# Both steps of the gated delta rule inverted level by level together, four groups at once, and the convolution's taps spread over twice as many turns

## The chip, the cores and the metric

One core of a Trainium2 chip runs the kernel. The metric is the device time of one execution in microseconds (us). Engines are named as in the profile: PE (TensorE, matmuls and transposes), DVE (VectorE), ACT (ScalarE), POOL (GpSimd), and SP, which only issues DMAs. Each engine works through its own list of instructions strictly in order; they meet at semaphores.

## What is computed

Two transformer blocks on 256 tokens of width 1024. The first has two layers (`DEPTH` = 2) with a hybrid mixer each; the change is in that mixer:

```
def hybrid_mixer(x, ...):
    proj = x @ w_in
    p_conv, p_q, p_k, p_v, p_dn, p_z, p_b, p_a = split_projection(proj)
    c = c_lin * jax.nn.sigmoid(c_gate)
    c = depthwise_conv(c, conv_dw) + conv_dw_b            # 31 taps, 256 channels
    y_conv = jax.nn.silu(layer_norm(c, ...)) @ conv_pw
    y_diff = differential_attention(q, k, v, lam, ...)    # 4 heads
    y_dn = gated_deltanet_bidir(p_dn, p_z, p_b, p_a, ...) # 4 heads, forward and backward
    return jnp.concatenate([y_conv, y_diff, y_dn], axis=-1) @ w_o
```

The delta rule is solved in blocks ("steps") of 128 tokens. For each step, direction and head a triangular 128x128 matrix has to be inverted. The inverse X is built up in seven levels (`LEVELS` = 7): level k takes the part LM of the matrix L that a constant mask of level k selects, and computes P = LM·X, then X − X·P, then the transpose of the new X. Layer 1 is followed by a feed-forward net, layer 2 by eight experts; a second block follows.

## The kernel before

**Groups.** The four heads of one step and one direction are a group, held in one PSUM bank as 4 x 128 columns. There are four groups in a layer: i = 2·step + dr. Before the change two `Group` objects (one for each direction) serve both steps, so step 1 can begin only when step 0's buffers are free.

**Threads and turns.** Each engine's list for the mixer is written by `weave`, which takes one piece in turn from each of three generators: `mixer_attention`, `mixer_delta`, `mixer_conv`. A `yield` ends a piece. I call one round of `weave` a turn and count turns from 0; turn n of one engine belongs to turn n of the others. Nothing else decides the order: inside a turn attention comes first, then delta, then conv.

**Delta on PE** (`invert`): k = 0 transposes LM (L809). Each level k from 1 takes three turns, each for both directions: P = LM·X (8 matmuls, L759), then X·P (L759), then the transposes of X (L838). ACT copies P and the transpose out of PSUM (L2141), DVE subtracts X·P from X (L1314), and POOL makes the next level's LM with `mask` (L2622). Before the first level POOL also makes `XT` = 1 − LM and the first mask, four operations for each pair of groups. The delta thread takes 50 turns: begin 2, products 2, scaled 2, invert 18, solved 1, begin 2, then products and invert of step 1 (20 turns, with state(0) and scaled(1) beside them), solved 1, state(1) 2.

**Attention**: turns 0 to 3 project the keys (L567, w_in slice at ring use `MIX[l]`+4), turns 4 to 7 the values and the rotated heads' transposes (L574). From turn 8 each of the eight head-and-tile pieces i has its turn of `scores(i)` (L676; turn 8 + 3i), and in the turn after it `turn_mix(i-1)` (L574, which needs DVE's mixing of i-1), and in the third turn `out` (L567). On DVE, in the turn of scores(i): the maxima of scores(i) (L1517), then the mixing of i-1 (L1524, L1317, L1314, L1320). From turn 41 PE does pieces of the output projection (L720).

**Convolution** on DVE: 30 taps for two halves, 60 operations (L1320 on b_cols), four a turn, so 15 turns. They are followed on PE by two sums (L567 with b_cst 128x256) and by the pointwise matmuls (L567 with b_pw), with DVE, POOL and ACT in between.

**Weights** come through four ring slots (`ring`), in the order of `uses`; SP waits for the readers of what lay in the slot, in that order. The slot of use `MIX[l]`+4 (the keys' weights) is next filled with the first weights of the feed-forward net or of the experts.

```
def weave(*threads):
    live = list(threads)
    while live:
        for g in list(live):
            try:
                next(g)
            except StopIteration:
                live.remove(g)
```

Of the kernel before, what the change touches and what calls it, by code (L numbers as in the profile page):

```python
# [238 lines left out]
class Views:  # L239


    def __init__(self, arena):
        self.arena, self.at = arena, 0

    def __call__(self, *shape):
        n = int(np.prod(shape))
        ap = self.arena[:, self.at:self.at + n]
        self.at += n
        assert self.at <= 23168, self.at
        return view(ap, *shape)  # L250


class Group:


    def __init__(self, A, XTf, n):
        self.LT, self.LM, self.P, self.X, self.XT = (A(4, 128) for _ in range(5))
        self.QT = [A(4, 128), view(XTf[:, 512 * n:512 * n + 512], 4, 128)]
        self.Rv, self.Rk, self.kd, self.U = (A(4, 64) for _ in range(4))
        self.wT, self.st, self.g4 = A(2, 128), A(2, 128), [A(16), A(16)]  # L260


def two_blocks(nc, a):
    ctx = ExitStack()
    with ctx:
# [24 lines left out]
        with nc.sbuf_tensor("b_arena", [128, 23168], F32) as arena:  # L290
            pass
# [51 lines left out]
        groups = [Group(A, XTf, n) for n in range(2)]  # L343
        q2 = view(flat(groups[0].P), 2, 256)
        r8 = groups[0].g4[0][:, 0:8]
# [74 lines left out]
        r_one, r_out = sig("r_one", 4), sig("r_out", 4)  # L420
# [62 lines left out]
        def mixer_uses(l):  # L483
# [5 lines left out]
            use(rows8(w, 1024, 512), k_rows(l, 1))  # L489
# [72 lines left out]
        def pe(e):  # L562
# [161 lines left out]
            def mixer_conv(l):  # L724
                for _ in range(15):
# [15 lines left out]
            def mixer_delta(l, done):  # L741
# [20 lines left out]
                def begin(step):  # L762
                    for dr in range(2):
                        i, t = 2 * step + dr, step if dr == 0 else 1 - step
                        G, tri, g4 = groups[dr], C(f"tri{dr}"), gz[:, t, 4 * dr:4 * dr + 4]
# [10 lines left out]
                def products(step):  # L776
                    for dr in range(2):
                        i, t = 2 * step + dr, step if dr == 0 else 1 - step
                        G = groups[dr]
# [16 lines left out]
                def scaled():  # L796
                    for dr in range(2):
                        yield

                def invert(step):  # L800
                    for k in range(LEVELS):
                        last = k == LEVELS - 1
                        for dr in range(2):
                            G, i = groups[dr], 2 * step + dr
                            b = B.take()
                            e.wait_ge(*masked(l, 14 * step + 2 * k + dr))
                            if k == 0:
                                for h in range(4):
                                    ins = e.transpose(heads(b)[:, h, :], G.LM[:, h, :], ident)  # L809
                                ins.then_inc(lm_turn.sem)  # L810
                                B.until(b, inv_X0(l, i))
                            else:
# [2112 lines left out]
```

## Time and profile before

| | |
|---|---|
| median of 3 runs | 2388.54 us (2385.37 to 2389.2) |
| profiled execution, its own time | 2390.41 us |
| its span | 2388.3 us |
| mean granted TensorE clock | 0.954 of full |
| PE, DVE, ACT, POOL busy | 91%, 59%, 48%, 54% of the span |

The two mixers' woven parts run from 76 to about 277 us and from 565 to about 768 us. The rest of the span is the feed-forward net, the experts and the second block, which are not touched. PE's busy time counts the modelled ends of matmuls, so what matters in the mixer is the gaps in it and what ended them.

### The profile page before, as it was taken

The numbers are of one execution on the slowest core, as the hardware profiler recorded it, in microseconds if no ns is written. First come the engines' busy times: TensorE is split into PE (matmuls) and PEld (weight loads), VectorE is DVE, ScalarE is ACT, GpSimd is POOL, SyncE is SP. The second block draws the span as 40 slices with busy tenths as digits, with TensorE's granted clock in tenths as the row PEclk, the third lists the DMA queues.
The fourth block names the chain that finished last, engine by engine and source line by source line (L and its number), as shares of the span: only waits on it lengthen the run. The fifth ranks groups of instructions, "written<-read, shape, count | busy, mean of one in ns | idle before, by whom it ended". The sixth has DMA issues, their size and how long they took to land.

```text
span 2388.3 us, 26921 instructions
## 1 busy us (share of the span) xinstructions
PE 2175.7 (91%) x10612; PEld 1742.4 (73%) x10612; DVE 1408.6 (59%) x1743; ACT 1144.9 (48%) x1164; POOL 1296.4 (54%) x555
## 2 busy tenths in 40 slices
PE   8988699989788599999999999999899996887997
PEld 7467488875675577787777777888778774647997
DVE  1774534345844477777777776433477775545665
ACT  1143244321431376767767675433376672534554
POOL 0333145502430398989989896455399891204453
PEclk9999899999989699999999999999999997978999
DMA  8210075433100499998989897445489893204550
GB/s 295 106 36 1 1 263 191 159 121 134 36 1 1 156 354 334 349 358 322 358 315 361 317 361 270 176 177 204 149 318 356 322 358 132 99 26 159 212 199 32
DMA packets 208097, 484.97 MB, mean 203 GB/s; under 512 B 9168, under 2 KB 13008, under 8 KB 206928
## 3 DMA queue, kind: packets, MB, share of 16 engines
q1 hardware_dynamic: 207952, 483.02, 55.9%
q8 instruction: 92, 1.51, 0.3%
q14 instruction: 53, 0.43, 0.1%
HBM read 481.96 MB, written 1.05 MB: 202 GB/s over the span
## 4 chain that ended last, share of the span: by engine, by line
PE 82%; DVE 11%; ACT 2%; issue 2%; SPq 1%; POOL 1%; DMA 1%; DVEq 0%; ACTq 0%
PE bank L938 20%; PE bank L940 20%; PE bank L939 20%; PE bank L567 10%; PE bank L759 4%; DVE b_arena L1320 3%; PE bank L574 3%; DVE b_arena L1314 2%; PE bank L720 1%; DVE b_X L1314 1%; ACT e_hi L2141 1%; PE bank L1207 1%; POOL e_lo L2762 1%; DMA b_ba<-in_w_in 1%; DVE b_arena L1317 1%
## 5 line engine op out<-in xcount | busy, mean ns | idle before, releaser
L2762 POOL TENSOR_TENSOR e_lo<-b_ring,e_hi 128x512 fp32r<-128x512 f32 (+2 forms) x407 | 1146.0, 2837 | 569.8 <-ACT e_hi L2141 569.8
L1772 DVE TENSOR_TENSOR e_lo<-b_ring,e_hi 128x1536 fp32r<-128x1536 f32 (+1 forms) x403 | 773.6, 1920 | 471.0 <-ACT e_hi L2141 467.7
L2141 ACT ACTIVATE e_hi<-b_ring 128x2048 fp32r<-128x2048 f32 (+1 forms) x407 | 776.4, 1911 | 367.5 <-PE bank L940 334.7
L938 PE MATMUL bank<-e_hi,e_xh 128*128 128x512 f32 (+1 forms) x1200 | 476.2, 397 | 30.8 <-issue 13.0
L940 PE MATMUL bank<-e_hi,e_xl 128*128 128x512 f32 (+1 forms) x1200 | 467.4, 390 | 0.0
L939 PE MATMUL bank<-e_lo,e_xh 128*128 128x512 f32 (+1 forms) x1200 | 466.7, 389 | 0.0
L938 PEld LDWEIGHTS bank<-e_hi,e_xh 128*128 128x128 f32 x1200 | 226.8, 189 | 97.5 <-issue 50.3
L938 PE MATMUL bank<-e_hi,e_th 128*128 128x512 f32 x688 | 272.2, 396 | 0.7
L940 PE MATMUL bank<-e_hi,e_tl 128*128 128x512 f32 x688 | 268.6, 390 | 0.0
L939 PE MATMUL bank<-e_lo,e_th 128*128 128x512 f32 x688 | 268.3, 390 | 0.0
L940 PEld LDWEIGHTS bank<-e_hi,e_xl 128*128 128x128 f32 x1200 | 226.9, 189 | 48.1
L939 PEld LDWEIGHTS bank<-e_lo,e_xh 128*128 128x128 f32 x1200 | 227.1, 189 | 42.2
L2622 POOL TENSOR_TENSOR b_arena<-b_arena,b_cst 128x512 f32<-128x512 f32 (+1 forms) x72 | 90.9, 1280 | 218.9 <-DVE b_arena L1314 121.0
L2141 ACT ACTIVATE b_arena<-bank 128x512 f32<-128x512 f32 (+2 forms) x164 | 87.1, 547 | 212.8 <-PE bank L574 80.0
L938 PEld LDWEIGHTS bank<-e_hi,e_th 128*128 128x128 f32 x688 | 129.1, 188 | 39.0 <-issue 11.2
L940 PEld LDWEIGHTS bank<-e_hi,e_tl 128*128 128x128 f32 x688 | 129.1, 188 | 27.9
L939 PEld LDWEIGHTS bank<-e_lo,e_th 128*128 128x128 f32 x688 | 129.3, 188 | 23.7
L759 PEld LDWEIGHTS bank<-b_arena 128*128 128x128 f32 (+1 forms) x928 | 120.5, 205 | 21.1 <-issue 15.6
L759 PE MATMUL bank<-b_arena 128*128 128x128 f32 (+1 forms) x928 | 132.3, 294 | 3.6 <-issue 1.6
L567 PE MATMUL bank<-b_ring,b_XT 128*128 128x512 f32 (+1 forms) x320 | 121.6, 532 | 2.4 <-issue 2.4
L2622 POOL TENSOR_TENSOR b_arena<-b_arena 128x256 f32<-128x256 f32 (+1 forms) x46 | 36.7, 821 | 157.6 <-ACT b_arena L2141 136.8
L938 PE MATMUL bank<-e_xh,e_hi 128*128 128x256 f32 x384 | 110.1, 287 | 1.4 <-DVE e_xl L1776 1.4
(214 smaller groups left out, 2426.4 us busy)
## 6 DMA issues: line engine op xcount, KB each, us to landing
b_ring<-in_moe_w SPq DMA_DIRECT2D x168, 2048.0 KB, 8.1
b_ring<-in_w_in SPq DMA_DIRECT2D x15, 2048.0 KB, 8.1
b_ring<-in_ffn_w SPq DMA_DIRECT2D x15, 2048.0 KB, 7.9
b_ring<-in_w_up SPq DMA_DIRECT2D x12, 2048.0 KB, 8.0
b_ring<-in_w_down SPq DMA_DIRECT2D x6, 2048.0 KB, 8.5
b_ring<-in_w_o SPq DMA_DIRECT2D x4, 2048.0 KB, 7.8
b_gain<-in_gains SPq DMA_DIRECT2D x7, 1024.0 KB, 4.9
b_ring<-in_w_out SPq DMA_DIRECT2D x2, 2048.0 KB, 8.3
```

The lines of the kernel that those rows point to most:

```text
L567: ins = e.matmul(out, x, y, start=start and i == 0, stop=stop and i == len(pairs) - 1)
L574: last = e.transpose(out[:, tok(j)], x, ident)
L759: last = e.matmul(heads(b)[:, h, :], *f(h), start=True, stop=True)
L938: e.matmul(out, ah, bh, start=first, stop=False)
L939: e.matmul(out, ah, bl, start=False, stop=False)
L940: return e.matmul(out, al, bh, start=False, stop=last)
L1314: return e.tensor_tensor(out, x, y, op)
L1320: return e.scalar_tensor_tensor(out=out, in0=x, scalar=s, in1=y, op0=o1, op1=o2)
L1772: e.tensor_tensor(lo[:, 0:at], raw[:, 0:at], r32(hi[:, 0:at]), ALU.subtract).then_inc(lo_dve.sem)
L2141: return e.activation(out, x, ACT.Copy)
L2622: return e.tensor_tensor(out, x, y, op)
L2762: e.tensor_tensor(lo[:, at:], raw[:, at:], r32(hi[:, at:]), ALU.subtract).then_inc(lo_pool.sem)
```

## The change

The `Group` objects become four for each layer: two in the arena, and two whose four large tiles lie in the ring slot of the keys' weights and whose XT lies in the first half of `b_XT`. Both steps' `begin` and `products` come first (turns 0 to 7), then one `invert` for all four groups: each level has two turns of P (step 0's pair, then step 1's), two of X·P, two of transposes. `solved`, `state(0)` and `state(1)` follow. That makes 49 turns. On POOL `scaled` is dealt out into the X·P turns. The taps come two a turn, in 30 turns, and what follows them is 15 turns later. The ring slot is now filled again only after the last X·P (`inv_XP(l)`).

```diff
@@ second groups, in the ring slot and in XT
+        first = [Group([A(4, 128) for _ in range(4)], A(4, 128), A) for _ in range(2)]
+        def second(l):
+            r = ring[(MIX[l] + 4) % NR]
+            return [Group([view(r[:, 2048 * n + 512 * i:2048 * n + 512 * i + 512], 4, 128) for i in range(4)],
+                          view(XTf[:, 512 * n:512 * n + 512], 4, 128), B, first[n]) for n in range(2)]
@@ mixer_uses
-            use(rows8(w, 1024, 512), k_rows(l, 1))
+            use(rows8(w, 1024, 512), inv_XP(l))
@@ pe, mixer_conv
-                for _ in range(15):
+                for _ in range(30):
@@ pe, mixer_delta (DVE, ACT and POOL alike)
-                def invert(step):
+                def invert():
                     for k in range(LEVELS):
                         last = k == LEVELS - 1
-                        for dr in range(2):
...
-                        yield
+                        for step in range(2):
+                            for dr in range(2):
+                                i = 2 * step + dr
+                                G, n = groups[l][i], 4 * (k - 1) + i
+                                b = B.take()
+                                e.wait_ge(*masked(l, 4 * k + i))
...
+                            yield
@@
-                yield from begin(0)
-                yield from products(0)
-                yield from scaled()
-                yield from invert(0)
-                yield from solved(0)
-                yield from begin(1)
-                yield from turns(middle(), tail())
-                yield from solved(1)
+                for step in range(2):
+                    yield from begin(step)
+                    yield from products(step)
+                yield from invert()
+                yield from solved()
+                yield from state(0)
                 yield from state(1)
@@ dve, mixer_conv
-                    if i % 2:
-                        yield
+                    yield
@@ pool, mixer_delta
                         if step:
-                            e.wait_ge(*X_out(l, 10 + dr))
+                            e.wait_ge(*k_rows(l))
...
+                    rest = scaled()
...
+                                if k == 0:
+                                    G = groups[l][i]
+                                    if step:
+                                        e.wait_ge(*v_rows(l))
+                                    e.wait_ge(*masked(l, i))
+                                    tt(G.XT, id4, G.LM, ALU.subtract).then_inc(inv_XT0.sem)
+                                    e.wait_ge(*lm_turn(l, i))
+                                    e.wait_ge(*inv_XT0(l, i))
+                                    mask(i, 1)
+                                elif not last:
+                                    e.wait_ge(*inv_P(l, 4 * (k - 1) + i))
+                                    mask(i, k + 1)
+                            yield
...
+                        for step in range(2):
+                            next(rest, None)
+                            yield
```

How PE's list reads in layer 1, within level k = 2. Before, from the two products P over the turn of scores to `turn_mix` (L759 is a product, L676 the scores, L574 `turn_mix`; both directions come in each place):

```order
L759 MATMUL bank<-b_arena 128x128 [waits s_X_out,s_masked]
L759 MATMUL bank<-b_arena 128x128 x3
L759 MATMUL bank<-b_arena 128x128 [waits s_X_out,s_masked]
L759 MATMUL bank<-b_arena 128x128 x3
L676 MATMUL bank<-b_arena 128x256 [waits s_s_exp]
L676 MATMUL bank<-b_arena 128x256 [waits s_score]
L759 MATMUL bank<-b_arena 128x128 [waits s_XT_out,s_P_out]
L759 MATMUL bank<-b_arena 128x128 x3
L759 MATMUL bank<-b_arena 128x128 [waits s_XT_out,s_P_out]
L759 MATMUL bank<-b_arena 128x128 x3
L574 MATMUL bank<-b_cst,b_arena 128x128 [waits s_s_mix,s_s_exp]
L574 MATMUL bank<-b_cst,b_arena 128x128
```

After, one turn of scores among the transposes (L690 is the scores, L852 the transposes, L588 `turn_mix`):

```order
L690 MATMUL bank<-b_arena 128x256 [waits s_s_exp]
L690 MATMUL bank<-b_arena 128x256 [waits s_score]
L852 MATMUL bank<-b_cst,b_arena 128x128 [waits s_X_out]
L852 MATMUL bank<-b_cst,b_arena 128x128 x3
L852 MATMUL bank<-b_cst,b_arena 128x128 [waits s_X_out]
L852 MATMUL bank<-b_cst,b_arena 128x128 x3
L588 MATMUL bank<-b_cst,b_arena 128x128 [waits s_s_mix,s_s_exp]
L588 MATMUL bank<-b_cst,b_arena 128x128
```

Between scores and `turn_mix` there stood always the two X·P products; now there stand in turn the two P products of step 1's pair and, as here, the two short transposes.

On POOL, from the first masks to the first level, before (each operation on 128x512 takes the same form; L2622 is every tensor operation of POOL):

```order
L2622 TENSOR_TENSOR b_arena<-b_cst,b_arena 128x512 [waits s_masked]
L2622 TENSOR_TENSOR b_arena<-b_arena,b_cst 128x512 [waits s_inv_XT0,s_lm_turn]
L2622 TENSOR_TENSOR b_arena<-b_cst,b_arena 128x512 [waits s_masked]
L2622 TENSOR_TENSOR b_arena<-b_arena,b_cst 128x512 [waits s_inv_XT0,s_lm_turn]
L2622 TENSOR_TENSOR b_arena<-b_arena,b_cst 128x512 [waits s_inv_P] x8
```

and after:

```order
L2610 TENSOR_TENSOR b_ring0<-b_ring0,b_cst 128x512 [waits s_L_out] x2
L2610 TENSOR_TENSOR b_arena<-b_cst,b_arena 128x512 [waits s_masked]
L2610 TENSOR_TENSOR b_arena<-b_arena,b_cst 128x512 [waits s_inv_XT0,s_lm_turn]
L2610 TENSOR_TENSOR b_arena<-b_cst,b_arena 128x512 [waits s_masked]
L2610 TENSOR_TENSOR b_arena<-b_arena,b_cst 128x512 [waits s_inv_XT0,s_lm_turn]
L2610 TENSOR_TENSOR b_XT<-b_cst,b_ring0 128x512 [waits s_masked,s_v_rows]
L2610 TENSOR_TENSOR b_ring0<-b_ring0,b_cst 128x512 [waits s_inv_XT0,s_lm_turn]
L2610 TENSOR_TENSOR b_XT<-b_cst,b_ring0 128x512 [waits s_masked,s_v_rows]
L2610 TENSOR_TENSOR b_ring0<-b_ring0,b_cst 128x512 [waits s_inv_XT0,s_lm_turn]
```

Eight such operations now stand in one row behind the last mask of `products`, where four stood in each of two places.

On DVE, between two turns of scores, before (L1517 the maxima, L1320 on b_cols the taps):

```order
L1320 SCALAR_TENSOR_TENSOR b_arena<-b_arena,b_cols 128x251 [waits s_dve_order] x2
L1320 SCALAR_TENSOR_TENSOR b_arena<-b_arena,b_cols 128x250 [waits s_dve_order] x2
L1320 SCALAR_TENSOR_TENSOR b_arena<-b_arena,b_cols 128x249 [waits s_dve_order] x2
L1517 TENSOR_REDUCE b_arena<-bank 128x2 [waits s_score]
L1317 TENSOR_SCALAR b_arena<-b_arena 128x2 [waits s_dve_order]
L1524 RECIPROCAL b_arena<-b_arena 128x2 [waits s_s_exp]
```

and after:

```order
L1326 SCALAR_TENSOR_TENSOR b_arena<-b_arena,b_cols 128x255 [waits s_dve_order] x4
L1541 COPY b_arena<-bank 128x128 [waits s_att_sq]
L1326 SCALAR_TENSOR_TENSOR b_arena<-b_arena,b_cols 128x254 [waits s_dve_order] x2
L1523 TENSOR_REDUCE b_arena<-bank 128x2 [waits s_score]
L1323 TENSOR_SCALAR b_arena<-b_arena 128x2 [waits s_dve_order]
L1530 RECIPROCAL b_arena<-b_arena 128x2 [waits s_s_exp]
```

There are six taps between two scores instead of twelve.

## Rows read from the trace of the kernel before

**Rows 1.** First line of the profile's page
```profile
span 2388.3 us, 26921 instructions
```

**Rows 2.** Busy time in stretches, both mixers; start:end, length, each engine
```profile
core 0: us, PE busy (x) PEld busy (x) DVE busy (x) ACT busy (x) POOL busy (x), PEclk, DMA share, GB/s
...
76.00:277.00 201.00, 175.79 (x975) 128.74 (x976) 116.69 (x255) 59.10 (x139) 61.97 (x58) 0.96 0.09 32
565.00:768.00 203.00, 178.04 (x980) 129.65 (x980) 116.65 (x258) 59.08 (x139) 63.30 (x58) 0.96 0.09 32
```

**Rows 3.** PE's waits in the first mixer (75 to 277 us): total, times, longest
```profile
PE bank L574 <- DVE b_arena L1320: 8.5, 5, 2.8
PE bank L574 <- DVE b_arena L1314: 4.6, 2, 3.4
PE bank L574 <- ACT b_arena L2240: 2.7, 1, 2.7
```

**Rows 4.** Timeline of PE, turns 5 and 6: start, length, idle before
```profile
111.19 1.97 PE L574 MATMUL bank<-b_cst,b_arena 128*128 128x128 f32 x8 [3.35 <-DVE b_arena L1314]
...
118.28 1.10 PE L574 MATMUL bank<-b_cst,b_arena 128*128 128x128 f32 x8 [1.23 <-DVE b_arena L1314]
```

**Rows 5.** Timeline of PE, level 2 of step 0
```profile
130.01 1.23 PE L838 MATMUL bank<-b_cst,b_arena 128*128 128x128 f32 x8 [1.18 <-DVE b_arena L1314]
131.07 1.95 PE L759 MATMUL bank<-b_arena 128*128 128x128 f32 x16
132.95 1.45 PE L676 MATMUL bank<-b_arena 64*128 64x256 f32 x4
134.33 2.05 PE L759 MATMUL bank<-b_arena 128*128 128x128 f32 x16
...
139.18 0.41 PE L574 MATMUL bank<-b_cst,b_arena 128*128 128x128 f32 x2 [2.79 <-DVE b_arena L1320]
```

**Rows 6.** Timeline of DVE: taps, then a mixing's last operation
```profile
82.86 1.61 DVE L1320 SCALAR_TENSOR_TENSOR b_arena<-b_arena,b_cols 128x241 f32<-128x241 f32 x4
...
121.06 7.41 DVE L1320 SCALAR_TENSOR_TENSOR b_arena<-b_arena,b_cols 128x253 f32<-128x253 f32 x8
...
130.38 6.80 DVE L1320 SCALAR_TENSOR_TENSOR b_arena<-b_arena,b_cols 128x254 f32<-128x254 f32 x12
...
138.54 0.48 DVE L1320 SCALAR_TENSOR_TENSOR b_arena<-b_arena 128x256 f32<-128x256 f32 x1
```

**Rows 7.** Timeline of POOL: before the first level, then two masks
```profile
118.66 1.27 POOL L2622 TENSOR_TENSOR b_arena<-b_cst,b_arena 128x512 f32<-128x512 f32 x1
...
122.92 1.27 POOL L2622 TENSOR_TENSOR b_arena<-b_arena,b_cst 128x512 f32<-128x512 f32 x1
124.66 2.74 POOL L2622 TENSOR_TENSOR b_arena<-b_arena,b_cst 128x512 f32<-128x512 f32 x2 [0.47 <-PE bank L759]
```

**Rows 8.** Timeline of PE: scores and `turn_mix` with no taps on DVE
```profile
181.44 1.45 PE L676 MATMUL bank<-b_arena 64*128 64x256 f32 x4
...
185.00 0.41 PE L574 MATMUL bank<-b_cst,b_arena 128*128 128x128 f32 x2 [0.59 <-DVE b_arena L1320]
```

**Rows 9.** Timeline of DVE, a mixing while POOL works (197 to 201 us)
```profile
197.37 0.69 DVE L1517 TENSOR_REDUCE b_arena<-bank 128x2 f32<-128x512 f32 x1
...
198.46 0.59 DVE L1317 TENSOR_SCALAR b_arena<-b_arena 128x256 f32<-128x256 f32 x1
198.98 0.56 DVE L1314 TENSOR_TENSOR b_arena<-b_arena,b_sc 128x1 f32<-128x1 f32 x1
199.57 1.45 DVE L1320 SCALAR_TENSOR_TENSOR b_arena<-b_arena 128x256 f32<-128x256 f32 x1
```

**Rows 10.** Timeline of PE: the `turn_mix` behind that mixing
```profile
201.17 0.41 PE L574 MATMUL bank<-b_cst,b_arena 128*128 128x128 f32 x2 [2.82 <-DVE b_arena L1320]
```

**Rows 11.** Timeline of PE: the convolution's second sum, and its pointwise product
```profile
159.70 1.03 PE L567 MATMUL bank<-b_arena,b_cst 128*128 128x256 f32 x4
...
168.35 1.97 PE L567 MATMUL bank<-b_arena,b_pw 128*128 128x256 f32 x8 [0.55 <-ACT b_arena L2144]
```

**Rows 12.** Timeline of SP's queue: the first feed-forward weights
```profile
96.90 27.18 SPq L2809 DMA_DIRECT2D b_ring<-in_ffn_w  x2
```

**Rows 13.** Timeline of PE: the mixer's last product, and what follows
```profile
272.42 7.13 PE L567 MATMUL bank<-b_ring,b_arena 128*128 128x512 f32 x16 [0.47 <-ACT b_arena L2141]
```

**Rows 14.** The page's DMA issues: KB of one, us to landing
```profile
b_ring<-in_ffn_w SPq DMA_DIRECT2D x15, 2048.0 KB, 7.9
```

More of the change, by code:

```diff
@@ L841, in invert @@
-                        yield
+                        for step in range(2):
+                            for dr in range(2):
+                                G, n = groups[l][2 * step + dr], 4 * (k - 1) + 2 * step + dr
+                                b = B.take()
+                                e.wait_ge(*X_out(l, n))
+                                for h in range(4):
+                                    ins = e.transpose(heads(b)[:, h, :], G.X[:, h, :], ident)
+                                ins.then_inc(inv_turn.sem)
+                                B.until(b, XT_out(l, n))
+                            yield
@@ L2340, in invert, with solved @@
-                        yield
-                def solved(step):
-                    for dr in range(2):
+                        for step in range(2):
+                            for dr in range(2):
+                                b = B.take()
+                                e.wait_ge(*inv_turn(l, 4 * (k - 1) + 2 * step + dr))
+                                copy(groups[l][2 * step + dr].XT, heads(b)).then_inc(XT_out.sem)
+                            yield
+                def solved():
+                    for i in range(4):
@@ L2359, in state @@
                     yield
-                def tail():
-                    yield from state(0)
-                    yield from scaled()
-                def middle():
-                    yield from products(1)
-                    yield from invert(1)
-                yield from begin(0)
-                yield from products(0)
-                yield from scaled()
-                yield from invert(0)
-                yield from solved(0)
-                yield from begin(1)
-                yield from turns(middle(), tail())
-                yield from solved(1)
+                for step in range(2):
+                    yield from begin(step)
+                    yield from products()
+                yield from invert()
+                yield from solved()
+                yield from state(0)
                 yield from state(1)
@@ L2724, in invert @@
                         yield
[L2726 to L2746 removed]
+                        yield
+                for step in range(2):
+                    yield from begin(step)
+                    yield from products(step)
+                yield from invert()
             def mixer(l):
```

341 lines of the change are left out of this document (149 added, 192 removed).

## The prediction, made before the changed kernel had run

> **What bounds the kernel now.** The page's first line gives the span, 2388.3 us [rows 1]; the execution's own time was 2390.41 us, 1.9 us above the median of the runs (2388.54). Next I read busy time by stretches, to see which engine leaves how much open in the part that the change touches. In the first mixer PE is busy 175.8 of 201 us and in the second 178.0 of 203 [rows 2], no other engine above 117. So PE has some 25 us of gaps in each mixer. The products that it does are the same ones after the change, and the number of turns goes only from 50 to 49. The whole effect is therefore what becomes of about 25 us of gaps in each of two layers (and of the clock within them): even with all of it gone the kernel would be 50 us faster, and a part of it (the start, the tail) is not touched.
>
> The third view is who ended PE's waits. The largest entries of the first mixer are waits for DVE, and they stand in front of L574 [rows 3]: the attention's `turn_mix` and the rotated heads, not the inversion. In front of the inversion's own products stand few. In other words, the dependency chain of the inversion (PE, ACT, PE, DVE, PE) is already covered, by the two directions and the attention piece of each turn. What is not covered is the attention's own chain: scores on PE, maxima and mixing on DVE, `turn_mix` on PE in the next turn.
>
> The timeline shows how. In a level with taps, scores run from 132.95, the two X·P products to 136.4, and then PE is idle for 2.79 us, until DVE has mixed [rows 5]; in that time DVE was still in twelve taps, 6.80 us from 130.38 on [rows 6]. Where DVE has no taps in front, `turn_mix` starts 2.1 us after the end of scores (182.89 to 185.00) [rows 8]. That 2.1 us is the bare chain. X·P for two directions lasts 2.05 us [rows 5], so before the change it covers the bare chain almost exactly, and only taps make a gap of it.
>
> **The change, term by term**, for one mixer, in us of PE idle time. I replay PE's list turn by turn with the durations of the rows.
>
> *Front, turns 0 to 7.* Before: gaps of 0.84 at the start, 3.35 and 1.23 [rows 4], 5.4 in all. After, the rotated heads still wait for DVE in turn 5 (same chain, 3.4). Behind them comes `begin(1)`, whose wide copy on POOL now stands behind POOL's two rotary operations; these start when PE's wait ends and take 2.8, the copy 0.6, while PE has 2.3 of work: a gap of 1.1. In turn 6 the second rotary wait has `begin(1)`'s four DVE operations in front of it: 1.6 in place of 1.23. Sum 7.0, so +1.6. Bounds: 0 (POOL and DVE quick enough) and +3.
>
> *Start of the levels.* POOL needs four operations for each pair of groups (XT and mask), 5.5 us from 118.66 to 124.19 [rows 7]. Now eight stand in a row behind the last mask of `products`, which can start only about when turn 7 ends: 1 + 11.1 us. PE's work from there to the end of the fourth P is 1.45 (scores), 2.1 (transposes), 1.95, 1.45, 1.95 = 8.9 [rows 5]; its last product waits for POOL's last mask. Gap 4.2. Before, step 0's wait was covered by the values' projection, and step 1's was mostly paid by a `turn_mix` wait of 2.8 [rows 10] and 1.7 behind it. Bounds: 2.5 and 6.
>
> *Scores among P.* Four turns of scores (i = 1, 3, 5, 7) now have the two P products behind them, 1.95 us, nearly the bare chain: 0.4 would be left. But at that time POOL is making masks: each P product that ends starts one, 2.74 for two [rows 7]. The trace shows what DVE's mixing costs beside POOL: the three operations from 198.46 on take 0.59, 0.56 and 1.45 [rows 9], where the last alone takes 0.48 [rows 6], and PE's gap behind it was 2.82 with 1.1 us of cover [rows 10]. That is 1.6 us more than the bare chain. Taps show the same: 1.61 for four with POOL idle, 7.41 for eight with POOL at work [rows 6]. Before, masks were over when the mixing began, since they belong to the turn ahead. I take 2.0 for each, 8.0 in all; bounds 0.4 each (no meeting with POOL) and 2.4.
> The Trainium skill bears on this (SBUF — State Buffer, section "Who interferes with whom"): a DVE instruction with two SBUF inputs and a GpSimd instruction that reads SBUF exclude each other for a whole instruction. By that rule the mixing's two operations of this kind could each wait for a whole mask and these four gaps be near 3 us each, 4 us more in a mixer than I take; the rows, which show 1.6 us, decide here.
>
> *Scores among transposes.* The other turns (i = 2, 4, 6) have the two transposes as their only cover, 1.04 to 1.23 us [rows 5] where X·P stood: 1.1 of the bare chain is left open, and DVE comes 0.25 late from the subtraction of the last X·P and two taps. I take 1.35, the first 0.5 more: 4.5. Bounds 3 and 8.
>
> *What the taps gave.* With six taps and not twelve between two scores, DVE is no longer behind in the levels: the waits of 2.79 and 2.7 and smaller ones go. Before, all gaps between turn 8 and the tail sum to 16.6 (24.5, the sum of the wait list, less 5.4 at the front and 2.5 in the tail). All of these are taken away and replaced by the terms here.
>
> *Behind the taps.* The pointwise product waits for a chain from the second sum's end (160.6 to 168.35, 7.8 us) [rows 11], in which ACT loads two tables. PE had 7.3 of work in that time and a gap of 0.55; after, the turns are two single-pair P, one transposition and no scores, 5.8: gap 2.0 (bounds 0.5 and 2.5). The norm of the attention rows stays as it is, at 2.2.
>
> *Tail.* `state(0)` moves from the middle to the end: PE's work is only moved, one wait of 0.4 is added; 2.9 in place of 2.5.
>
> *The ring slot.* The first weights of the next stage were issued at 96.9 [rows 12] and will be issued after the last X·P, near 255. Two loads, which share this queue and its order, need 2 x 7.9 us to land [rows 14], so about 271; the mixer's last product ends at 279.6 [rows 13] and only then does ACT begin to split them. Zero; if that cover were gone it would be up to 16 us once in each layer.
>
> Sum after: 7.0 + 4.2 + 8.0 + 4.5 + 2.0 + 2.2 + 2.9 = 30.8, against 24.5: **+6.3 a mixer, +12.6 in all.** Against its own time 2390.4 + 12.6 = 2403.0, and 1.9 below that for the median: **2401 us**. The bounds of all terms at once give 18 to 40, that is -13 to +31 in all, but they do not fall together.
>
> The clock: the granted clock is 0.96 over each mixer [rows 2]. At two levels, 1.2 and 2.4 GHz, that is 8% of 201 us, 16 us, at the lower one, which lost 8 us. They lie behind the gaps of 2.7 us and more (the first L574 of rows 4 took 1.97, the second, of the same form, 1.10). After, single gaps are smaller but more of them; I take the same loss.
>
> **Rivals.**
> 1. *Faster.* The gaps among P come out at 0.4 since the mixing slips between two masks (-13 for both layers: no change), and in addition the clock stays high, since only two gaps above 2.7 are left in a mixer (up to -8 in each). Time 2378. For it: gaps of 2.8 disappear and PE is evenly loaded at 80%. Against it: the rows of POOL and DVE at 198 us, and the long gap at the start of the levels. Chance 0.22.
> 2. *No change.* Half of this: gaps of 1.2 among P, or a third of the clock's loss back. 2389. Chance 0.18.
> 3. *Much slower.* DVE falls behind in the turns after the start, where POOL works without a break for 11 us and slows the taps to 0.9 each; each later turn_mix starts late, and gaps of 3 bring the clock down in the levels: 8 us more in each mixer. 2418. For it: eight taps took 7.41. Against it: DVE has half the taps. Chance 0.08.
> 4. *The weights come late.* SP's queue holds the second load behind the first, and both now wait for the inversion. It decides once they land after 279.6, that is with 8 us more than I count: 2410 to 2430. Chance 0.02.
> My forecast (slower by 0.25 to 0.9%) has 0.50.
>
> **From these to the numbers.** The likeliest case's own range is 2394 to 2410. To leave out no more than 2 in 10 it has to take in the second case and most of the first: 2378 to 2413. A measurement of this kernel can tell about 0.2%, 4.8 us, from no change. Faster 0.22, within it 0.18, slower 0.60.
>
> **What the changed profile would show.** Woven parts of some 207 us and 209 us with PE busy as before and about 31 of gaps. PE's waits still led by L588 (`turn_mix`) for DVE, with more and smaller entries: seven in each mixer of 1.2 to 2.4. On POOL eight operations in a row, and behind them two PE waits at the first P products. DVE's stretches of 6.8 us of taps gone. In the mixing among P, a last operation of 1.2 to 1.45; if it is 0.48 there, rival 1 gains. Granted clock about 0.96 in the mixers; at 0.99 the forecast is wrong by 8 to 12 us. The ffn weights issued near 255 us and no new wait of ACT behind the mixer.

## The result, and the profile after

The changed kernel takes 2399.53 us (median of 5 runs, 2398.31 to 2404.46) against 2388.54 (2385.37 to 2389.76, 5 runs): 11 us slower. The ratio estimated from all the runs is 1.0052, 95% interval 1.0038 to 1.0067. The forecast was slower, 2401 us. The profiled execution took 2398.31 us of its own.

The page's first line, and busy time over the woven parts; each stretch runs from the mixer's first product behind the 0.84 us wait to the start of its last (L581 here, L567 in [rows 13]). Columns as in [rows 2]:

```profile
span 2396.2 us, 26907 instructions
...
76.12:279.38 203.26, 170.58 (x964) 127.60 (x965) 123.88 (x253) 55.43 (x137) 57.87 (x51) 0.94 0.09 32
572.09:773.39 201.30, 169.19 (x964) 126.37 (x964) 123.82 (x253) 55.22 (x137) 57.90 (x51) 0.95 0.09 32
```

Cut the same way, the parts of before are 196.3 and 194.9 us, with PE busy 171.2 and 170.9. PE's work has not grown; the gaps in it have. The sum of the gaps that the timeline marks is 31.6 and 31.1 us now and was 23.8 and 22.7. PE's waits in the first mixer, 75 to 285 us, which answer to [rows 3]:

```profile
PE bank L588 <- DVE b_arena L1326: 17.3, 8, 5.8
PE bank L581 <- ACT b_arena L2140: 3.6, 1, 3.6
PE bank L588 <- DVE b_arena L1320: 3.2, 1, 3.2
PE bank L773 <- DVE b_arena L1320: 2.6, 1, 2.6
PE bank L773 <- POOL b_ring L2656: 2.0, 2, 1.7
```

`turn_mix` (L588) waiting for DVE's mixing (L1326) leads, with twice what the same wait had before. Where each gap stands, in PE's timeline:

```profile
112.70 1.09 PE L588 MATMUL bank<-b_cst,b_arena 128*128 128x128 f32 x8 [3.18 <-DVE b_arena L1320]
116.02 2.05 PE L773 MATMUL bank<-b_cst,b_ring 128*128 128x128 f32 x8 [1.73 <-POOL b_ring L2656]
...
140.62 3.27 PE L773 MATMUL bank<-b_arena 128*128 128x128 f32 x16 [2.64 <-DVE b_arena L1320]
...
153.76 0.66 PE L588 MATMUL bank<-b_cst,b_arena 128*128 128x128 f32 x2 [5.81 <-DVE b_arena L1326]
...
163.37 0.41 PE L588 MATMUL bank<-b_cst,b_arena 128*128 128x128 f32 x2 [1.10 <-ACT b_arena L2236]
...
172.42 0.41 PE L588 MATMUL bank<-b_cst,b_arena 128*128 128x128 f32 x2 [2.17 <-DVE b_arena L1326]
...
222.49 3.19 PE L581 MATMUL bank<-b_arena,b_pw 128*128 128x256 f32 x8 [3.58 <-ACT b_arena L2140]
...
233.56 1.08 PE L588 MATMUL bank<-b_cst,b_arena 128*128 128x128 f32 x4 [2.54 <-DVE b_arena L1326]
```

From 163 us on the gaps alternate, 1.10 among the transposes and 2.17 or 2.18 among the products P, three of each. The second mixer has the same list to within 0.2 us, except that the 1.73 is 0.74 there. What is new in the size is the 5.81. DVE's timeline in front of it, then a mixing among P (168 to 172 us):

```profile
142.88 1.27 DVE L1320 TENSOR_TENSOR b_ring<-b_cst,bank 128x512 f32<-128x512 f32 x2
144.08 5.73 DVE L1326 SCALAR_TENSOR_TENSOR b_arena<-b_arena,b_cols 128x250 f32<-128x250 f32 x4
149.73 0.68 DVE L1523 TENSOR_REDUCE b_arena<-bank 128x2 f32<-128x512 f32 x1
...
169.56 1.22 DVE L1320 TENSOR_TENSOR b_arena<-b_arena,b_sc 128x1 f32<-128x1 f32 x1
170.82 1.45 DVE L1326 SCALAR_TENSOR_TENSOR b_arena<-b_arena 128x256 f32<-128x256 f32 x1
```

and POOL's timeline over the same times:

```profile
144.06 1.26 POOL L2610 TENSOR_TENSOR b_XT<-b_cst,b_ring 128x512 f32<-128x512 f32 x1
145.46 1.26 POOL L2610 TENSOR_TENSOR b_ring<-b_ring,b_cst 128x512 f32<-128x512 f32 x1
146.69 2.85 POOL L2610 TENSOR_TENSOR b_arena<-b_arena,b_cst 128x512 f32<-128x512 f32 x2
149.50 2.65 POOL L2610 TENSOR_TENSOR b_ring<-b_ring,b_cst 128x512 f32<-128x512 f32 x2
...
169.44 2.55 POOL L2610 TENSOR_TENSOR b_ring<-b_ring,b_cst 128x512 f32<-128x512 f32 x2 [0.47 <-PE bank L773]
```

A tap takes 0.40 us with POOL idle (1.61 for four, [rows 6]) and 1.43 here, where POOL runs without a pause: one DVE operation for each of POOL's. An operation on one element a row (128x1), 0.15 us elsewhere, takes 1.22 at 169.56 and ends as POOL's first mask of that pair does; the next ends 0.3 us after the second mask. DVE's subtractions that read PSUM (x2 in 1.27) are not slower.

### The profile page after: what moved, and what is told of

Its sections match the earlier page's. It is cut to its first block, busy times and chain, and to the rows that moved or that the text cites. A ratio compares the mean times of both kernels' runs of the same rounds, so it can differ in the third digit from the quotient of the medians.

```text
span 2396.2 us, 26907 instructions
## 1 busy us (share of the span) xinstructions
PE 2166.2 (90%) x10612; PEld 1736.7 (72%) x10612; DVE 1426.3 (60%) x1743; ACT 1138.0 (47%) x1162; POOL 1287.1 (54%) x543
## 4 chain that ended last, share of the span: by engine, by line
PE 81%; DVE 11%; issue 2%; POOL 2%; ACT 2%; SPq 1%; DMA 1%; DVEq 0%; ACTq 0%; POOLq 0%
PE bank L944 20%; PE bank L946 19%; PE bank L945 19%; PE bank L581 11%; PE bank L773 3%; PE bank L588 3%; DVE b_arena L1326 2%; DVE b_arena L1320 2%; POOL b_arena L2610 1%; PE bank L734 1%; ACT e_hi L2137 1%; DVE b_X L1320 1%; POOL e_lo L2742 1%; PE bank L1213 1%; DVE b_arena L1323 1%
## 5 line engine op out<-in xcount | busy, mean ns | idle before, releaser
L2610 POOL TENSOR_TENSOR b_arena<-b_arena,b_cst 128x512 f32<-128x512 f32 (+1 forms) x44 | 55.5, 1282 | 167.1 <-DVE b_arena L1320 99.1
L2137 ACT ACTIVATE b_arena<-bank 128x512 f32<-128x512 f32 (+2 forms) x120 | 60.3, 529 | 166.9 <-PE bank L588 61.2
L581 PE MATMUL bank<-b_ring,b_XT 128*128 128x512 f32 (+1 forms) x320 | 125.8, 545 | 2.4 <-issue 2.4
L2610 POOL TENSOR_TENSOR b_arena<-b_arena 128x256 f32<-128x256 f32 (+1 forms) x34 | 26.3, 786 | 166.0 <-ACT b_arena L2137 136.8
L946 PE MATMUL bank<-e_xh,e_lo 128*128 128x256 f32 x384 | 108.7, 283 | 0.0
L945 PE MATMUL bank<-e_xl,e_hi 128*128 128x256 f32 x384 | 108.7, 283 | 0.0
```

The costliest lines, as they stand in the source:

```text
L581: ins = e.matmul(out, x, y, start=start and i == 0, stop=stop and i == len(pairs) - 1)
L945: e.matmul(out, ah, bl, start=False, stop=False)
L946: return e.matmul(out, al, bh, start=False, stop=last)
L2137: return e.activation(out, x, ACT.Copy)
L2610: return e.tensor_tensor(out, x, y, op)
```

## The experiments

All times are medians beside the kernel before on the same chip (its medians there were 2388.1 to 2390.0); the ratio is estimated from the runs of both and is not exactly that of the medians. The woven parts, their gaps, PE's busy time and its granted clock in them are from the profiled execution of each, first and second mixer. The last column is the rest of that execution's span, where no edit changes what the engines do.

| | us | ratio to before (95%) | woven parts | gaps | PE busy | clock | rest |
|---|---|---|---|---|---|---|---|
| before | 2388.54 | | 196.3, 194.9 | 23.8, 22.7 | 171.2, 170.9 | 0.96, 0.96 | 1997.1 |
| changed | 2399.53 | 1.0052 (1.0038 to 1.0067) | 203.3, 201.3 | 31.6, 31.1 | 170.6, 169.2 | 0.94, 0.95 | 1991.6 |
| e1 | 2385.63 | 0.9992 (0.9980 to 1.0004) | 197.2, 199.0 | 17.9, 19.6 | 177.5, 177.6 | 0.91, 0.91 | 1995.1 |
| e2 | 2411.5 | 1.0093 (1.0076 to 1.0109) | 206.6, 208.6 | 33.3, 31.0 | 172.4, 176.7 | 0.93, 0.91 | 1993.8 |
| e3 | 2382.89 | 0.9966 (0.9954 to 0.9979) | 192.7, 192.3 | 21.0, 20.5 | 170.2, 170.5 | 0.95, 0.95 | 1999.2 |
| e4 | 2392.95 | 1.0017 (1.0006 to 1.0028) | 196.0, 197.5 | 24.8, 25.6 | 170.1, 170.9 | 0.95, 0.95 | 1996.2 |
| e5 | 2403.82 | 1.0053 (1.0037 to 1.0069) | 199.8, 200.2 | 30.1, 30.1 | 168.7, 169.1 | 0.95, 0.94 | 2005.2 |
| e6 | 2388.86 | 0.9990 (0.9978 to 1.0001) | 191.7, 190.8 | 23.3, 22.9 | 167.4, 166.9 | 0.96, 0.96 | 2000.1 |
| e7 | 2373.05 | 0.9926 (0.9913 to 0.9938) | 188.4, 188.7 | 20.5, 20.7 | 167.0, 167.0 | 0.97, 0.97 | 1996.9 |
| e8 | 2382.71 | 0.9972 (0.9961 to 0.9982) | 191.1, 191.6 | 20.9, 20.7 | 169.4, 169.9 | 0.96, 0.96 | 1993.8 |
| e9 | 2373.35 | 0.9934 (0.9921 to 0.9947) | 185.8, 190.2 | 21.4, 20.9 | 163.4, 168.4 | 0.98, 0.96 | 2003.0 |
| e10 | 2385.22 | 0.9981 (0.9972 to 0.9989) | 189.8, 190.1 | 20.0, 20.2 | 168.9, 168.9 | 0.96, 0.96 | 1996.3 |
| e11 | 2372.73 | 0.9942 (0.9927 to 0.9957) | 187.6, 188.8 | 17.7, 18.9 | 169.0, 168.9 | 0.96, 0.96 | 1993.6 |
| e12 | 2372.09 | 0.9925 (0.9909 to 0.9942) | 185.2, 185.2 | 18.9, 18.6 | 165.3, 165.5 | 0.97, 0.97 | 1999.7 |

Two columns are easy to overlook. PE does the same products in all rows, yet its busy time goes from 163 to 178 us with the clock that it is granted, so a woven part can shrink or grow without its gaps. And the rest, which no edit touches, differs by up to 13.6 us between the profiled executions, more than the change costs; a difference of a few us between two medians says little of the woven parts unless the profile shows it there.

The theory was that of the prediction: the joint inversion costs by what it puts beside what. A `turn_mix` gets less cover on PE, and its mixing on DVE now meets POOL's masks. The rivals were that the dependency chain of the inversion itself or the clock sets the time.

**The change in halves.** e1 is the kernel before with the taps alone spread:

```diff
-                    if i % 2:
-                        yield
+                    yield
@@ pe, mixer_conv
-                for _ in range(15):
+                for _ in range(30):
```

> The kernel before, with the taps alone changed: two a turn in 30 turns, and what follows them 15 turns later; the two steps are still inverted one after the other. My theory: PE's gaps in the mixer are waits for the attention's mixing on DVE, and before the change the taps made those at 139 and 149 us (2.8, 2.7), with 0.8 and part of 1.2 beside them. Then this half of the change is a gain: some 4.5 us less of gaps in each mixer, 2379 to 2382 us. Rival A (the taps sat in time that DVE had to spare): 2388. Rival B (the taps only move: they now slow DVE in the start of step 1's levels, where POOL is busy, and the scores of turn 29): 2386 to 2392, with a longer wait than 2.8 at that place.

The time is unchanged, close to rival B, whose longer wait came as well. The gaps of [rows 5] and their like are gone and two new ones are there, 3.62 (a mixing beside POOL's operations at the start of step 1's levels) and 3.65 (a subtraction behind DVE's chain for the convolution's norm). The gaps are still 5.9 us less in the first mixer and 3.1 in the second, but PE's busy time rose from 171.2 to 177.5 and from 170.9 to 177.6: the granted clock ate the gain (last section).

e2 is the changed kernel with that edit undone, four taps a turn in 15 turns:

> The changed kernel with the taps alone undone: four a turn in 15 turns. My theory: the joint inversion alone is what costs, and the taps' spreading had taken part of it back, so this is slower still: DVE has four taps a turn in the start of the levels, where POOL slows each to about 1.4 us, so the gap of 5.8 us there grows by 3 to 6; later turns have no taps and gain 0.3 each. 2403 to 2410 us. Rival (taps are innocent in the changed kernel): 2398 to 2401.

12 us slower than the changed kernel, slower than the forecast of 2403 to 2410. The gaps at the start of the levels are 5.44 and 6.63 in place of 2.64 and 5.81, and the next is 2.80. The last waits behind scores are those of the changed kernel (2.19, 1.10, 2.18), but one gap among transposes and the 3.58 in front of the pointwise product, which comes earlier here, are gone. In sum the gaps are 33.3 and 31.0, only 1.7 us more in the first mixer and none in the second, while the woven parts are 3.3 and 7.3 us longer, at a clock of 0.93 and 0.91 and with PE busy 1.8 and 7.5 us more. So the joint inversion alone costs some 22 us, and the spread taps take half of that back, but less through the gaps, as my theory had it, than through the clock.

**Do the masks cause the gaps among P?** e3 is the changed kernel with the masks of levels 2 to 6 made one element wide, so that the products of those levels use what lies in LM already:

```diff
+                    if k > 1:
+                        tt(G.LM[:, 0, 0:1], G.LT[:, 0, 0:1], C(f"m{1 - i % 2}{k}")[:, 0:1], ALU.mult).then_inc(masked.sem)
+                        return
                     tt(G.LM, G.LT, M, ALU.mult).then_inc(masked.sem)
```

> The changed kernel with POOL's masks of levels 2 to 6 reduced to one element each, in place of 128x512; so it leaves out that part of the computation (the inverse is wrong), and POOL is nearly idle in the levels. It tells whether the gaps of 2.2 us behind scores among P are made by POOL's masks beside DVE's mixing. My theory: they fall to 0.4 to 0.6 (the bare chain of 2.1 less 1.95 of P products), and the gap of 5.8 by 1 to 3; those of 1.1 behind scores among transposes stay. 2384 to 2390 us. Rival (the chain itself is that long and POOL has no part): gaps stay at 2.2, 2399.

PE's gaps in it, 152 to 206 us:

```profile
152.53 0.41 PE L588 MATMUL bank<-b_cst,b_arena 128*128 128x128 f32 x2 [3.03 <-DVE b_arena L1326]
...
161.73 0.41 PE L588 MATMUL bank<-b_cst,b_arena 128*128 128x128 f32 x2 [1.17 <-ACT b_arena L2236]
...
176.67 0.41 PE L588 MATMUL bank<-b_cst,b_arena 128*128 128x128 f32 x2 [1.10 <-DVE b_arena L1326]
...
191.62 0.41 PE L588 MATMUL bank<-b_cst,b_arena 128*128 128x128 f32 x2 [1.10 <-DVE b_arena L1326]
```

The time falls by 17 us below that of the changed kernel. The three gaps of 2.17 are gone and nothing stands in their place: with POOL out of the way the two products P cover the bare chain. Those among the transposes keep their 1.10, so they are a matter of cover alone. The first falls from 5.81 to 3.03; what is left is XT and the masks of level 1, which e3 leaves as they are.

**More cover.** e4 puts `turn_mix` one turn later on PE, and ACT's copy of its result with it; `out(i-2)` takes the turn that it leaves, on DVE and ACT too. DVE's mixing stays. The cut shows the order on PE:

```diff
                     yield
-                    if 1 <= i < 9:
-                        turn_mix(i - 1)
-                    yield
                     if i >= 2:
                         out(i - 2)
                     yield
+                    if 1 <= i < 9:
+                        turn_mix(i - 1)
+                    yield
```

> The changed kernel with one thing moved: on PE and ACT the attention's out(i-2) comes in the turn behind scores(i), and turn_mix(i-1) one turn later (DVE's copy of out a turn earlier). So two turns of the delta rule stand between scores and turn_mix. My theory: the seven waits in the levels are one chain with too short a cover; with 3 to 4 us of cover the gaps of 2.2 and 1.1 vanish and 5.8 falls to 2 or 3. 12 to 14 us less in each mixer: 2371 to 2376 us, below both kernels. Rival (DVE is behind in all, so the wait only moves to X_out or to the next scores): 2386 to 2396, with new waits of 1 to 2 us at the transposes.

The gaps fell by 6.8 and 5.5 us where I had expected 12 to 14 in each mixer, and the time by 7 us in all:

```profile
153.96 0.41 PE L592 MATMUL bank<-b_cst,b_arena 128*128 128x128 f32 x2 [4.03 <-DVE b_arena L1330]
...
178.06 0.41 PE L592 MATMUL bank<-b_cst,b_arena 128*128 128x128 f32 x2 [1.58 <-DVE b_arena L1330]
```

The small gaps are fewer and 1.0 to 1.6 long, not gone, and DVE now works from 166 to 205 us with two pauses of 0.5. I read that as DVE itself being the bound there, with taps and mixing stretched by POOL: four taps take 3.66 at 179.40 and 3.63 at 195.62, for 1.61 with POOL idle. e5 attacks the start in another way. It inverts level 0 of step 0's pair between `begin(1)` and `products(1)`, so that four of POOL's eight operations come earlier:

```diff
-                for step in range(2):
-                    yield from begin(step)
-                    yield from products(step)
-                yield from invert()
+                yield from begin(0)
+                yield from products(0)
+                yield from begin(1)
+                yield from invert(0)
+                yield from products(1)
+                yield from invert(1)
+                yield from invert(2)
```

> The changed kernel with level 0 of step 0's pair (transposes on PE, XT and first mask on POOL, X on DVE) moved from turn 8 to turn 6, between begin(1) and products(1), where POOL is idle for some 10 us; only four of the eight POOL operations then stand behind the last mask of products. It measures the term for the start of the levels. My theory: the gap of 2.6 before the first P goes, and the 5.8 behind it falls to about 3, since POOL blocks DVE for 5.5 us less: 5 us in each mixer, 2388 to 2392 us. Rival (the 5.8 is DVE's own backlog and not POOL's row): only 2.6 goes, 2394 to 2396.

The 2.64 in front of the first P is gone, the 5.80 stays, with the same four taps in 5.73 us in front of it, beside a row of POOL's that is still unbroken there. The time came out above both expectations: it is the same as the changed kernel's within its scatter (2395.8 to 2408.6). The woven parts are 4.6 us shorter in all; the rest of the profiled execution is 13.5 us longer, so the time can't be held against the edit. e6 has both edits:

> Both moves on the changed kernel: turn_mix a turn later and level 0 of step 0's pair in turn 6. If the two act on different gaps, their gains add: 2392.9 less some 9, 2382 to 2386 us, about 0.2% below the kernel before. If DVE is what bounds the levels by now (it was without a pause from 167 to 203 us in the kernel with turn_mix later), what the start gives is lost again in the levels: 2389 to 2392.

In the time they bring back what the change had cost, and no more; the woven parts are 8.7 us below those of before in all, and the rest of the profiled execution 3.0 above. The 4.03 is still there.

**The same slack without the joint inversion.** e7 is e1 with `turn_mix` a turn later, e8 the kernel before with only that:

> The kernel before with the taps spread over 30 turns and turn_mix a turn later; the two steps are inverted one after the other. Of the kernel with the taps alone (2385.6) the waits of 1.0 and 3.6 us of L574 go; the new one of 3.65 before L838 (DVE held by the convolution's chain) stays. My theory: 3 to 4.5 us less in each mixer, 2377 to 2380 us, below both kernels; it would say that the joint inversion gives nothing that a turn of slack does not give. Rival: the wait moves to DVE's subtraction behind the mixing, 2384 to 2387.

> The kernel before with turn_mix a turn later alone, taps four a turn. Two readings of the waits of 2.8 and 2.7 us: DVE was full there (twelve taps, mixing and subtractions sum to 9.6 of the 9.7 us of a level), so that slack cannot help in those levels and only the 2.8 at 201 us goes: 2382 to 2385. Or the chain was only late by its place: then all L574 waits go, 2374 to 2378.

e7 is 17 us faster than before and 26 faster than the changed kernel. Nothing in it is new but two orders: taps at half the rate, `turn_mix` a turn later. Each alone brings little (e1 nothing that can be told, e8 7 us, where its first reading had it, though 3.38 and 3.47 now stand where 2.79 and 2.82 stood and it is the 2.7 that is gone). The profile of e7 has 14.1 us of the gain in the woven parts, and only 5.4 of them are gaps: most of it is PE's busy time, 4.2 and 3.9 us less, at a clock of 0.97 for 0.96. Its largest gaps are now 4.67 at the first P of step 1's levels and 3.68 behind the convolution's chain.

**Taps away from POOL's row.** e9 is e6 with the taps dealt out by hand: four a turn in turns 0 to 7, none in turns 8 to 11, two a turn from 12 to 25. e10 is e7 with four a turn in turns 0 to 7 and two in turns 8 to 21. e11 is e10 with the reciprocal, the silu and the pointwise product behind the taps one turn later each.

```diff
-                    yield
+                    if i > 15 or i % 2:
+                        yield
+                    if i == 15:
+                        for _ in range(4):
+                            yield
```

> The joint inversion with what the runs so far point to: turn_mix a turn later, level 0 of step 0's pair early, and the taps dealt four a turn in turns 0 to 7, none in turns 8 to 11 (where POOL has its eight operations in a row), then two a turn until turn 25; their sum stays at turn 30. Theory (both inversions at once cost only through what meets on DVE and POOL; the chain of the inversion itself was covered before): the gap of 4.0 to 5.8 us at the first turn_mix falls to about 1, PE's gaps in a mixer come to about 17, the woven part to 188 and 189 us, the time to 2376, level with the step-after-step kernel that has the same two edits (2373) and not below it. Rival A (the joint inversion is worth something of its own once the collisions are gone): woven parts of 184 or less, 2366 or less. Rival B (DVE is the bound between turns 12 and 25, wherever the taps stand): the gap moves behind turn 12 and the time stays at 2384 to 2392.

> The kernel before (step after step) with turn_mix a turn later and the taps four a turn in turns 0 to 7, two a turn in turns 8 to 21, none afterwards; their sum stays at turn 30. Against the same kernel with two taps a turn in all 30 turns (2373.05). Theory: the gap of 4.7 us at the first product of step 1's levels is DVE behind in taps while POOL has its four operations for the step; without taps there it falls to 1 or less: woven parts of about 185 us in place of 188.5, time 2367. Rival (the four taps a turn meet POOL's operations for step 0 in turns 4 to 9 and cost the same there): the gap moves to the first level, time 2371 to 2376.

> As the kernel with the taps in turns 0 to 21 (e10), and in addition what follows the convolution's sums is drawn out: DVE's reciprocal, ACT's silu and PE's pointwise product come one turn later each. Theory: the 3.7 us gap of an inversion's transpose behind DVE's chain for the convolution's norm falls by 1 to 2.5, since the chain no longer sits in one turn ahead of the subtraction: 2 to 5 us below e10. Rival: the operation that holds DVE is in the first of these turns, ahead of the edit, and the gap stays: within 1.5 us of e10.

e9: the gap of 4.03 is 1.15, and the time is near the theory (2373, level with e7), though 21 us of gaps are left where I expected 17; rival B fell. Of the 15.5 us by which its median is below e6's the profiles show 6.0 and 0.5 in the woven parts. e10: missed. The gap went from 4.67 to 3.48 only, and the time is 12 us above e7. DVE's timeline in front of that gap (the product starts at 189.63) has no tap in it:

```profile
186.94 1.45 DVE L1324 SCALAR_TENSOR_TENSOR b_arena<-b_arena 128x256 f32<-128x256 f32 x1
188.32 1.27 DVE L1318 TENSOR_TENSOR b_arena<-b_cst,bank 128x512 f32<-128x512 f32 x2
```

The subtractions that the product needs stand behind a mixing that POOL slows; taps were a quarter of it. And the woven parts are only 1.4 and 1.3 us longer than e7's: of the 12 us most lie outside the parts that any edit touches (the two profiled executions are only 2.1 us apart). e11 took the 3.68 down to nothing (0.27) and a 0.95 came in front of the pointwise product, 2.2 and 1.3 us of woven part, as expected; of the 12.5 us by which its median is below e10's the profiles show 6 in all, of which 3.5 are in the woven parts. The rest of the kernel, the same instructions in each, varies by several us with the clock it is granted. I can't say why e10 has it worse.

e12 is e9 with e11's edit:

> The joint inversion with the taps in turns 0 to 7 and 12 to 25 (e9, 2373.35), and in addition the drawn-out end of the convolution that took 2.7 us of gaps and 2.2 us of the woven part out of the step-after-step kernel (e11 against e10). Theory: the gap of 3.6 us in front of the pointwise product falls to 1.5 or less, the woven part from 185.8 to 183.5 us, the time by 2 to 5 us to 2369 (more, if the clock of what follows shifts, as from e10 to e11). Rival: a new wait takes its place (the pointwise product one turn later meets the norm of the attention rows, which now costs 2.5), woven part within 1 us of e9, time 2372 to 2375.

Busy time over its woven parts:

```profile
77.77:262.96 185.19, 165.29 (x964) 122.98 (x964) 119.39 (x253) 54.45 (x137) 56.22 (x52) 0.97 0.09 34
555.93:741.08 185.15, 165.54 (x965) 123.27 (x965) 119.35 (x253) 54.45 (x137) 56.18 (x51) 0.97 0.09 34
```

The 3.59 is 1.36 and the woven parts are the shortest of all, 11.1 and 9.8 us below before; the first is 0.6 us below e9's, less than expected. The time, 2372.09, is where the rival had it, not below e7's, e9's or e11's by anything that can be told.

## Why the prediction was right, step by step

The direction, the size and the main step held: PE's gaps grew by 7.8 and 8.4 us a mixer where +6.3 stood, and the gaps make up the whole growth of the woven parts. By term, first mixer, predicted and measured:

| term | predicted | measured |
|---|---|---|
| front | 7.0 | 0.84 + 0.23 + 3.18 + 1.73 = 6.0 |
| start of the levels | 4.2 | 2.64 |
| scores among P | 4 x 2.0 = 8.0 | 5.81 + 3 x 2.17 = 12.3 |
| scores among transposes | 4.5 | 3 x 1.10 + 0.18 = 3.5 |
| pointwise product | 2.0 | 3.6 |
| norm of the attention rows | 2.2 | 2.5 |
| tail | 2.9 | 1.9 |
| sum | 30.8 | 32.5 |

- **Cover and POOL.** Three of the four gaps among P are 2.17 or 2.18 for the 2.0 that I took from [rows 9, 10], and e3 takes them away by taking the masks away. This step is shown. The 2.0 was the 1.6 of the rows and 0.4 for the bare chain; the rows of that gap give 1.7 (3.84 from the end of scores to `turn_mix`, less 2.1), and 2.1 less 1.95 of cover is 0.15, not 0.4: e3 shows no gap at all there. By the Trainium skill (SBUF — State Buffer, section "Who interferes with whom") a DVE operation with two SBUF inputs and an operation of POOL that reads SBUF shut each other out. The trace agrees in kind: both mixing operations of that sort end within 0.3 us of one of POOL's masks. A gap near 3 was too high, since each waits only for what is left of the running mask: 1.07 and 0.97 us more than the 0.15 and 0.48 that they take alone.
- **The first of the four was mis-sized, 5.81 for 2.0.** The step that failed is in my rival 3: taps beside POOL's unbroken row at 0.9 each, from eight in 7.41 [rows 6]. That stretch had pauses of POOL in it; without one a tap takes 1.43. What I gave 8 in 100 and 8 us a mixer thus happened for a single turn, for 3.6 us. DVE did catch up after it, as the half rate of taps let one expect.
- **Start.** POOL's row begins at 134.6 and the product waits for DVE's subtraction, not for POOL's last mask; 2.64 for 4.2, and one wait where I wrote two. The two terms at the start together are 8.5 for 6.2.
- **Front.** The second rotary wait that I counted as 1.6 is not there; `begin(1)`'s wide copy costs 1.73 for 1.1.
- **Pointwise product.** 3.6 for 2.0, above my bound of 2.5. From the second sum's end to the product it is 9.1 us now and was 7.8, while PE's work in it is 5.5 for the 5.8 of my replay. I had taken over the chain's length. ACT's part up to the end of its second table load is as long as it was (6.4 us), with the same copies in front of and between the loads; the 1.3 us are two waits behind it, for DVE:

```profile
220.34 0.60 ACT L2140 ACTIVATE b_arena<-b_arena,b_cols 128x256 f32<-128x256 f32 x1 [0.51 <-DVE b_arena L1320]
221.74 0.60 ACT L2140 ACTIVATE b_arena<-b_arena,b_cols 128x256 f32<-128x256 f32 x1 [0.80 <-DVE b_arena L1320]
```

DVE's two multiplications there, in the changed kernel with POOL's masks for step 1's pair beside them, then before and in e3:

```profile
219.12 2.59 DVE L1320 TENSOR_TENSOR b_arena<-b_arena 128x256 f32<-128x256 f32 x2
218.77 2.66 POOL L2610 TENSOR_TENSOR b_ring<-b_ring,b_cst 128x512 f32<-128x512 f32 x2
...
166.39 0.76 DVE L1314 TENSOR_TENSOR b_arena<-b_arena 128x256 f32<-128x256 f32 x2
...
211.37 0.76 DVE L1320 TENSOR_TENSOR b_arena<-b_arena 128x256 f32<-128x256 f32 x2
```

Without the masks, in e3, they take 0.76 again and the gap is 2.17: this is POOL once more, met in a place that I had not counted. e12 shows that a turn more is worth 2.2 us.
- **Ring slot.** The load is issued at 251.9 and no wait of ACT behind the mixer has come. Zero, as said:

```profile
251.93 0.99 SPq L2789 DMA_DIRECT2D b_ring<-in_ffn_w  x2
```

- **Clock.** I took the same loss. The granted clock is 0.94 and 0.95 for 0.96, PE's busy time slightly less than before, and the woven parts grew by 7.0 and 6.4 us, about as the gaps did. Right for this change, and right by luck: e1 shows that 5.9 us of gaps can be lost to the clock whole, and e2 and e7 that it can double an effect. My reading that the low clock lies behind the gaps of 2.7 us and more does not hold in the kernel before either: behind its 2.79 PE kept the full clock, and behind a gap of 1.92, at 225.76, it ran at the lower level of 1.2 GHz:

```profile
226.00:228.00 2.00, 2.00 (x14) 0.65 0.02 4
228.00:230.00 2.00, 2.00 (x12) 0.50 0.00 0
```

- **The whole.** The profile puts 13.4 us into the woven parts, but only 7.9 lie between the two profiled executions (2398.31 and 2390.41), since the untouched rest came out 5.5 us shorter in that one. The medians say 11.0; the sum said 12.6. With a rest that differs by as much as 13.6 us between profiled executions, so close a hit is in part luck.

Is the joint inversion worth anything in itself? With the same slack and every collision treated as far as I got, its woven parts are 2.4 and 3.6 us shorter than those of the step-after-step kernel (e12 against e11), though with 1.2 us more of gaps in the first mixer and 0.3 less in the second: what they gain is PE's busy time, 3.7 and 3.3 us less at a clock of 0.97 for 0.96. In the time of the kernel that is nothing (2372.09 and 2372.73). It stays open whether a better deal of the taps would bring more.

## What to carry to other kernels

When several independent threads are woven into one list for each engine, look first at which engine pairs meet in a turn and at how much work the consumer has between a request and its use. One turn of slack for the wait that leads the list and a thinner spread of the filler work (here the taps) brought 17 us, where the rebuilt inversion with the same thinner spread cost 11. Before laying long runs of GpSimd work on the path, move VectorE's work from SBUF to other turns, or the filler becomes the wait: with the taps out of POOL's row the gap there went from 4.03 to 1.15 (e9). And compare PE's busy time and the rest of the kernel as well as the gaps; in e7 and e2 more than half of what an order of work gave or took was clock.

## What the runs showed that I had not expected

- **The clock can fall without a long wait.** In e1 the granted clock was 0.50 from about 177 us on, and the last gap in front of it was 1.01 us; before it PE had done the small products of `begin(1)` (128x4) and of 64 rows. Busy time of PE in stretches of 5 us in e1 (start:end, length, PE busy, clock):

```profile
170.00:175.00 5.00, 3.93 (x26) 1.00 0.00 0
175.00:180.00 5.00, 4.88 (x25) 0.71 0.00 0
180.00:185.00 5.00, 5.00 (x24) 0.50 0.01 3
185.00:190.00 5.00, 4.94 (x20) 0.50 0.00 0
```

and over the same products in the kernel before, where that gap was 0.59 [rows 8]:

```profile
185.00:190.00 5.00, 4.88 (x33) 1.00 0.02 3
190.00:195.00 5.00, 4.94 (x40) 1.00 0.00 0
```

The same happened in the second mixer of e1 at the same place. PE looks fully busy at half speed, so the loss does not show as a wait; it cost e1 6.3 and 6.7 us, more than the 5.9 and 3.1 that it had won in gaps. No run shows what in this stretch brings it about.
- **Size does not protect from POOL.** A VectorE operation on one element a row took 1.22 us beside POOL and 0.15 without, eight times as much, while the operations that read PSUM beside the same masks kept their 0.69. Nor does a single input from SBUF: the mixing's TENSOR_SCALAR on 128x256 takes 0.35 us at 212.52, with POOL idle, and 1.24 at 151.06, in POOL's row.
